# Three instead of four plain FFN chunks per layer, and an earlier first pair of weight panels, in a one-core encoder step

## The reference

```python
def swiglu(x, g, w_gu, w_down):
    gu = rmsnorm(x, g) @ w_gu
    return (jax.nn.silu(gu[..., :D_FF]) * gu[..., D_FF:]) @ w_down
```

## Time and profile before

| | us |
|---|---|
| median of 3 runs | 1208.22 |
| lowest, highest | 1208.21, 1208.87 |
| profiled execution, its own time | 1208.02 |
| its span from first to last instruction | 1206.3 |

### The profile page before, as it was taken

The page is one execution under the profiler, slowest core; times in us unless marked ns, Lnnn a source line. Parts: engine busy times, 40 slices in busy tenths (PEclk is TensorE's granted clock), DMA queues, the critical chain, the costliest instruction groups (busy, mean ns, idle before and its releaser), DMA issues.

```text
span 1206.3 us, 22717 instructions
## 1 busy us (share of the span) xinstructions
PE 1197.1 (99%) x8853; PEld 1152.8 (96%) x8853; DVE 979.7 (81%) x1585; ACT 641.6 (53%) x1136; POOL 78.5 (7%) x111
## 2 busy tenths in 40 slices
PE   8999999999999999999999999999999999999998
PEld 8998999999999999999987887899999999999998
DVE  5777458999999999976674777557999999999973
ACT  6657335455555555545672567434555555455543
POOL 2000000002001000102001100000001000100200
PEclk9999999999999999999999999999999999999999
DMA  7343222236334433526434110333134433532533
GB/s 249 108 140 105 71 78 83 74 89 136 106 88 113 121 97 91 133 80 173 137 107 140 57 41 2 105 88 88 53 101 115 120 97 94 130 105 80 131 85 105
DMA packets 195242, 124.08 MB, mean 103 GB/s; under 512 B 6339, under 2 KB 185891, under 8 KB 194880
## 3 DMA queue, kind: packets, MB, share of 16 engines
q1 hardware_dynamic: 183904, 103.30, 28.9%
q0 software_dynamic: 11040, 19.27, 7.4%
q10 hardware_dynamic: 192, 0.06, 0.0%
HBM read 106.70 MB, written 7.94 MB: 95 GB/s over the span
## 4 chain that ended last, share of the span: by engine, by line
PE 93%; DVE 3%; ACT 1%; DMA 1%; issue 1%; SPq 0%; DVEq 0%; ACTq 0%
PE ACCP L2016 28%; PE ACCP L2037 24%; PE MISC L2037 23%; PE ACCP L2173 3%; PE ACCP L2196 3%; PE ACCP L2366 2%; PE ACCP L2341 2%; PE MISC L2055 1%; PE MISC L2302 1%; PE MISC L2315 1%; DMA XR<-in_x_prompt 1%; PE MISC L2061 1%; PE ACCP L2078 1%; PE ACCP L2092 1%; DMA PC<-PC 0%
## 5 line engine op out<-in xcount | busy, mean ns | idle before, releaser
L1179 ACT ACTIVATE WH<-RAW 128x1024 fp32r<-128x1024 f32 (+2 forms) x149 | 144.2, 968 | 145.8 <-PE ACCP L2016 93.5
L1197 ACT ACTIVATE EH<-SB 128x1024 fp32r<-128x1024 f32 (+1 forms) x116 | 112.5, 970 | 163.2 <-DVE SB L1568 82.8
L1543 DVE TENSOR_TENSOR WL<-RAW,WH 128x1024 fp32r<-128x1024 f32 (+2 forms) x148 | 165.8, 1120 | 30.8 <-ACT WH L1179 29.7
L1574 DVE TENSOR_TENSOR EL<-SB,EH 128x1024 fp32r<-128x1024 f32 (+1 forms) x116 | 128.7, 1109 | 5.5 <-ACT EH L1197 3.7
L2037 PE MATMUL MISC<-BH,EH 128*128 128x288 f32 x360 | 106.7, 296 | 0.0
L2037 PE MATMUL ACCP<-BH,EH 128*128 128x288 f32 x360 | 106.6, 296 | 0.0
L2037 PE MATMUL MISC<-BL,EH 128*128 128x288 f32 x360 | 106.2, 295 | 0.0
L2037 PE MATMUL ACCP<-BL,EH 128*128 128x288 f32 x360 | 106.2, 295 | 0.0
L2037 PE MATMUL ACCP<-BH,EL 128*128 128x288 f32 x360 | 105.8, 294 | 0.0
L2037 PE MATMUL MISC<-BH,EL 128*128 128x288 f32 x360 | 105.8, 294 | 0.0
L2016 PE MATMUL ACCP<-XH,WH 128*128 128x288 f32 x480 | 104.1, 298 | 0.0
(11 more groups left out here) (411 smaller groups left out, 3432.0 us busy)
## 6 DMA issues: line engine op xcount, KB each, us to landing
RAW<-in_w_gu SPq DMA_DIRECT2D x88, 512.0 KB, 4.1
RAW<-in_w_down SPq DMA_DIRECT2D x48, 384.0 KB, 4.1
RAW<-in_w_in SPq DMA_DIRECT2D x16, 512.0 KB, 4.2
RAW<-in_w_mem_kv SPq DMA_DIRECT2D x16, 512.0 KB, 3.8
RAW<-in_w_out SPq DMA_DIRECT2D x16, 512.0 KB, 3.8
X<-PC POOLq DMA_DIRECT2D x48, 144.0 KB, 3.2
RAW<-in_w_down SPq DMA_DIRECT2D x16, 256.0 KB, 3.0
RAW<-in_w_kv SPq DMA_DIRECT2D x8, 512.0 KB, 3.6
```

Source lines behind the costliest of these rows:

```text
L1179: a.activation(panel_in(WH, w % SPLIT_SLOTS, p), panel_in(RAW, p % RAW_SLOTS, p), ACT.Copy).then_inc(split_ready(w, True)[0], 1)
L1197: a.activation(EH[:, first:first + n, 0:nh], mixtures(s)[:, first:first + n, 0:nh], ACT.Copy).then_inc(block_hi, n)
L1543: v.tensor_tensor(panel_in(WL, w % SPLIT_SLOTS, p), panel_in(RAW, p % RAW_SLOTS, p), panel_in(WH, w % SPLIT_SLOTS, p), ALU.subtract).then_ ...
L1574: v.tensor_tensor(EL[:, first:first + n, 0:nh], mixtures(s)[:, first:first + n, 0:nh], EH[:, first:first + n, 0:nh], ALU.subtract).then_in ...
```

## The change

`LEADS` becomes 3, so chunk 3 is made by a pair: a layer has six plain panels and one more pair, and the first stretch of pairs is now chunks 3, 4, 5, 6. The panels of the first pair are loaded behind the second plain panel (`load_first`), and they keep their two RAW slots until the first pair is split; the four plain panels after them take turns in the other two slots (`slot_of`). Three of the four mixtures of the first pair move to the front of the FFN's preparation on DVE, ahead of the first `prepare_scale`, and the fourth stands behind the second `prepare_scale` (`prepare_fourth`; its place in FIRST_SB overlaps ACC, which the norm's sum reads). The mixing of the first two hidden chunks (`mix_blocks`, `blocks_hi`, `blocks_lo`) leaves the plain stage: it goes to the second pair, that of chunks 2 and 3 to the third pair, that of 4 and 5 to the fourth pair. The low splits of the tokens (`lo`) move up; the seventh, `token_lo(6)`, goes into the first pair's step between the third and the fourth low split of its weights.

```diff
-    LEADS = 4
+    LEADS = 3
...
-                   (1, 0): [("mix", 3), ("mix", 6), ("hi", 1), ("hi", 2)],
-                   (1, 1): [("lo", 0), ("lo", 1), ("hi", 3), ("hi", 4)],
-                   (2, 0): [("lo", 2), ("lo", 3), ("blocks", k0), ("hi", 5), ("hi", 6)],
-                   (2, 1): [("lo", 4), ("lo", 5), ("pair", count["pair"]), ("blocks_hi", k0)],
-                   (3, 0): [("lo", 6), ("blocks_lo", k0)], (3, 1): []}
+                   (1, 0): [("mix", 3), ("mix", 6), ("hi", 1), ("hi", 2), ("lo", 0)],
+                   (1, 1): [("lo", 1), ("lo", 2), ("hi", 3), ("hi", 4)],
+                   (2, 0): [("lo", 3), ("lo", 4), ("hi", 5), ("hi", 6)],
+                   (2, 1): [("lo", 5)]}
...
                     steps.append(r_step)
+                    add("prepare_pair", k=count["pair"], s=r_step.s)
                     add("prepare_scale", layer=layer, k=0)
                     add("prepare_scale", layer=layer, k=1)
+                    add("prepare_fourth", k=count["pair"])
...
+                if (j, e) == (0, 1):
+                    first_pair = take("panel", 2)
+                    panel_shape.extend([(KC, P)] * 2)
+                    raw_free.extend([("pair", count["pair"])] * 2)
+                    add("load_first", p=first_pair, view=gate_of(LEADS), ys=up_of(LEADS))
...
+        for n in range(2):
+            slot_of[first_pair + 4 + n] = (first_pair + 2 + n) % RAW_SLOTS
...
-            if n == 1:
-                k = k0 + LEADS // 2 - 1
+            if n in (1, 2):
+                k = k0 + n - 1
...
-                if p >= RAW_SLOTS:
-                    sp.wait_ge(*raw_released(p - RAW_SLOTS))
+                if raw_before[p] is not None:
+                    sp.wait_ge(*raw_released(raw_before[p]))
...
                 elif s.kind == "prepare_pair":
                     first = steps_of_pair[s.k]
+                    dve.wait_ge(sq_free, s.s)
                     mix_1(first)
                     mix_3(first)
                     mix_2(first)
-                    mix_4(first)
+                elif s.kind == "prepare_fourth":
+                    mix_4(steps_of_pair[s.k])
...
                         dve.wait_ge(panel_used, s.before.q + 1)
-                        for n in range(4):
+                        for n in range(3):
                             mix_lo(s, n, 1)
+                        token_lo(s.layer, NB - 1)
+                        mix_lo(s, 3, 1)
                         mix_lo_22(s)
```

More of the change, by code:

```diff
@@ L160, in encoder_kernel @@
     panel_shape, splits, raw_free = [], [], []
+    slot_of = {}
     units_before, sq_of_norm, job_of_wide, branch_bank = {}, {}, [], {}
@@ L337, in feed_forward @@
         for n, (which, j, part) in enumerate(order):
-            i, p, w = take("pair"), take("panel", 2), take("split")
+            i, w = take("pair"), take("split")
             nk = KC if which == "gu" else PARTS[part][1] - PARTS[part][0]
-            panel_shape.extend([(nk, P)] * 2)
+            if n:
+                p = take("panel", 2)
+                panel_shape.extend([(nk, P)] * 2)
+                raw_free.extend([("pair", i)] * 2)
+            else:
+                p = first_pair
             splits.append(("pair", p, i))
-            raw_free.extend([("pair", i)] * 2)
             prev = steps_of_pair[i - 1] if n else None
@@ L360, in feed_forward @@
                 h=layer * FC + j if which == "gu" else None, prev=prev, nxt=n + 1 < len(order),
-                alone=n == 0, bank=n % 2, side=count["acc"] % 2, before=steps[-1] if n == 0 else None,
+                alone=n == 0, bank=n % 2, side=count["acc"] % 2, before=last_lead if n == 0 else None,
                 m=count["job"], g=count["acc"], made=made, k=k,
@@ L832, in moving_of @@
             return {"x": (XH, XL, xl_ready, T), "y": (HH, HL, yl_ready, T)}[kind]
+        raw_slot, raw_before, users = [], [], [[] for _ in range(RAW_SLOTS)]
+        for p in range(len(panel_shape)):
+            slot = slot_of.get(p, p % RAW_SLOTS)
+            raw_slot.append(slot)
+            raw_before.append(users[slot][-1] if users[slot] else None)
+            users[slot].append(p)
         def panel_in(slots, slot, p):
@@ L1041, in _ @@
                         sp.dma_start(yp[:, 2:TT, D - P:D], YST[1][:, 2:TT]).then_inc(y_last_stored, 16)
-                elif s.kind == "pair":
+                elif s.kind == "load_first" or s.kind == "pair" and not s.alone:
                     load(s.p, s.view)
@@ L1539, in split_lo, with token_lo @@
                     gate = WH[:, w % SPLIT_SLOTS]
-                    v.tensor_tensor(gate[:, :, FH:2 * FH], panel_in(RAW, p % RAW_SLOTS, p), gate[:, :, 0:FH],
+                    v.tensor_tensor(gate[:, :, FH:2 * FH], panel_in(RAW, raw_slot[p], p), gate[:, :, 0:FH],
                                     ALU.subtract).then_inc(lo_ready, 1)
                     return
-                v.tensor_tensor(panel_in(WL, w % SPLIT_SLOTS, p), panel_in(RAW, p % RAW_SLOTS, p),
+                v.tensor_tensor(panel_in(WL, w % SPLIT_SLOTS, p), panel_in(RAW, raw_slot[p], p),
                                 panel_in(WH, w % SPLIT_SLOTS, p), ALU.subtract).then_inc(split_ready(w, False)[0], 1)
+            def token_lo(layer, k):
+                dve.wait_ge(xmixed, 4 * (layer + 1))
+                dve.wait_ge(xc_hi, NB * layer + k + 1)
+                v.tensor_tensor(BL[:, k], BT[:, k], BH[:, k], ALU.subtract).then_inc(xc_lo, 1)
             def mix_1(s):
@@ L1933, in _ @@
                 elif s.kind == "prepare_lo":
-                    dve.wait_ge(xmixed, 4 * (s.layer + 1))
-                    dve.wait_ge(xc_hi, NB * s.layer + s.k + 1)
-                    v.tensor_tensor(BL[:, s.k], BT[:, s.k], BH[:, s.k], ALU.subtract).then_inc(xc_lo, 1)
-                elif s.kind == "prepare_blocks":
-                    mix_blocks(s.k)
-                elif s.kind == "prepare_blocks_lo":
-                    blocks_lo(s.k)
+                    token_lo(s.layer, s.k)
                 elif s.kind == "prepare_pair":
                     first = steps_of_pair[s.k]
+                    dve.wait_ge(sq_free, s.s)
                     mix_1(first)
```

12 lines of the change are left out of this document (6 added, 6 removed).

## The result

| | before | after |
|---|---|---|
| median of 9 runs, us | 1208.02 | 1211.24 |
| lowest, highest | 1207.29, 1208.90 | 1210.63, 1211.69 |
| profiled execution: own time, span | 1208.02, 1206.3 | 1211.69, 1210.0 |

The ratio after to before is 1.0027, with a 95% interval of 1.0017 to 1.0038: slower by 0.27%, 3.2 us. 1211.3 was predicted, in a range of 1208.5 to 1212.8. The profiled execution of after is the highest of its nine runs.

The account below looks back on a forecast made before the run. DVE, not PE, was taken to set the first stretch of pairs. Layer 0's 1.19 + 0.49 and layer 1's 0.89 + 0.49 gave +3.06 us; on the median of 1208.22 that is 1211.3 us, range 1208.5 to 1212.8.

Parts of the forecast that it names:

- Rival A: PE sets the time; DVE's lateness ends no PE wait: saving 2 x 1.58 us gives 1205.1; chance 0.13.
- The chunk's move: Layer 0: PE swaps 12.78 us for an 11.20 us pair, yet the first down pair comes 1.19 us later.
- Mixtures and loads at no cost: Before layer 0's first scale: 3.00 us of DVE idle hides three mixtures (1.9 us); panels land some 8 us early.
- Rival D: Panels land too late for the wait, mixtures push the scales by up to 1.9 us: 1211.3 to 1215; chance 0.02.
- Two intervals of 12.70: After the first pair's cross: two pairs with hidden mixing cost DVE 12.70 us each from cross to cross.
- rival B: DVE's 0.64 us idle takes up part of the low split, third sum ends no wait: about 1209.0; chance 0.12.
- The seventh low split: `token_lo(6)` in the middle of the first pair's step on DVE: adds 1.27 us, which nothing hides.
- Layer 0's first cross: End of the first pair's step on DVE: cross at 226.48, DVE then 1.5 us late.
- Rival C: ACT's splits come late too, 0.64 us per pair, up to 3.8 us: 1213 to 1215; chance 0.07.
- Layer 1: Layer 1's first down pair: 904.91 against 904.02, 0.89 us later; the second sum no longer meets the POOL DMA wait.
- Third sum: Fourth pair, before the first down pair: DVE makes it in place of a POOL DMA, 0.49 us more per layer.
- PE's waits: Third and fourth pair: PE waits for EL or `blocks_lo`, about 3.2 us in sum in each layer.

Follow-up runs that it names:

- the kernel with the move and without the two small terms: Changed kernel with `token_lo(6)` back in the plain stage and the fourth pair's sum by a POOL DMA: 1207.91 us, ratio to before 0.9999.
- the early half alone: Kernel before, still four plain chunks, with the first pair's panels loaded and mixed early, later panels' slots moved: 1207.68 us, ratio 1.0001.
- the early split: Changed kernel with the seventh low split, `token_lo(6)`, moved back into the plain stage: 1209.27 us.
- the next kernel: Changed kernel with the first two hidden chunks' mixing and low split on POOL, `token_lo(6)` in the plain stage, fourth pair's sum by POOL DMA: 1217.74 us.

## Why the prediction was right, point by point

**Who sets the stretch.** Right. More work on DVE there lengthens the kernel by as much, less work shortens it until ACT's order and PE's 11.20 are next, and with one mixing away PE runs three pairs without a wait. Rival A, by which PE would have saved 1.58 us a layer, is out. With it falls the 1205.1 by the rule of "Identifying the Most-Contended Engine" in the Trainium skill's "Perfetto Trace Analysis": the engine with the highest share of the whole span was not the one that set this stretch.

**The chunk's move.** Right, and clearer than I put it. The move takes 12.78 us of plain work from PE and adds one step of DVE, 12.70 us from cross to cross, so it is worth about nothing, and the kernel with the move and without the two small terms shows nothing. PE's 11.20 for a pair never enters the sum.

**Mixtures and loads at no cost.** Right. The first scale's idle is 1.20 us (about 1.1 was foreseen), no plain panel waits, the first pair begins at 213.22 (213.51), and the early half alone has the ratio 1.0001. Rival D is out.

**Two intervals of 12.70.** Right to 0.01 us, in both layers. The idle of 0.64 before the low split at 223.51 is still there, so rival B's way of making time up didn't happen.

**The seventh low split.** The sign and the size were right (1.27 us, nothing hides it), but I gave only half of the reason. It isn't only that DVE's work is consecutive: the place it left would now have cover, 0.95 us of waiting for ACT's EH, and the place it went to has none. Putting it back returns some 0.8 to 0.9 of its 1.27 in each layer, besides the wait for the DMA in layer 0.

**Layer 0's first cross.** This is the step that failed. I put it at 226.48 - 0.27 = 226.21 on this execution's clock; it came at 227.16. I had treated the POOL DMA as layer 1's affair, where the wait was listed, and there I was right that it vanishes. In layer 0 I put the wait for the landing at nothing and took no landing time at all. Before the change it landed 4.2 us after its issue there, and nobody waited. The chain of after shows the row that I left out:

```profile
219.18 7.58 DMA PC<-PC
...
227.16 0.75 DVE GU L1627
```

A landing as in layer 1 before (881.01 less 875.36, 5.65 us) would have been early enough. The 0.95 us too late is the whole of the difference in the layer's term, +2.14 for +1.19; the executions of the changed kernel differ in it (1.08 and 0.67 us of wait). Rival C's price came, 0.95 in place of 0.64, in one place of six and from a DMA, not from ACT.

**Layer 1.** +0.88 for +0.89.

**Third sum.** 0.49 a layer was predicted. The stretches behind the first down pair give 0.66 and 0.29, 0.95 for 0.98, and the runs without it 0.5 to 1.4 for both layers. The first down pair now shows the wait that I expected, 0.41 us for EL at 266.68.

**PE's waits.** Foreseen as 3.2 us a layer from the third pair on. In layer 0 PE reaches the first down pair at 262.48, where its own pace (213.22 + 11.44 + 3 x 11.20) gives 258.26, so 4.2 us late, the 3.25 and the DMA's 0.95. In layer 1, without the DMA's wait, it is 907.43 against 859.15 + 11.44 + 3 x 11.20 = 904.19, 3.24 us late. The waits listed up to there are shorter, 2.6 and 2.0 us, since a matmul is listed with 0.29 us and the next one starts 0.13 after it, so that part of each wait lies under a matmul's record. In layer 0 the waits begin one pair earlier than I said, with 0.23 us in the second pair; in layer 1 they begin in the third, as foreseen.

**The total.** That 1211.24 came so close to 1211.3 is in part luck. The four stretches behind the first scale sum to +3.97 us in the profiled execution of after, and to +3.51 in that of the changed kernel measured again, for the +3.06 predicted, mostly by the DMA that I had at nothing; and the median of before came out 0.20 lower with nine runs than with three. The interval of the ratio, 1.0017 to 1.0038, is 2.1 to 4.6 us wide in time and can't tell these sums apart.

**Still open.** It stays open why the sum's DMA in layer 0 took 7.0 to 7.6 us in the five profiled kernels that had the split in the first pair's step and issued that DMA as early as in after, and 5.2 to 5.3 in the two with three plain chunks that had it in the plain stage. In the first kind, the two panel loads are issued 0.6 and 0.2 us ahead of it, in the second 1.9 and 1.5. That loads under way go with a late sum can be seen within after: the sums of the second and third pair, of the same size and with no panel load under way, land 2.7 us after their issue in both layers. But the distance alone doesn't set the time: in layer 1 of after the loads also stand 0.6 and 0.2 us ahead, and the sum landed in 5.6; with 1.9 and 1.5 it is 4.1 to 4.2 us in layer 0 and 5.2 to 5.7 in layer 1 of kernels with four plain chunks. No run moved the loads and left the sum where it was. The DMA issues of the first pair's step, in after in layer 0, in layer 1, and with the early split in layer 0, and last the second pair's sum in layer 0 of after (median us to landing):

```profile
RAW<-in_w_gu SPq DMA_DIRECT2D x2, 512.0 KB, 6.1
PC<-PC POOLq DMA_DIRECT2D x1, 144.0 KB, 7.6
```

```profile
RAW<-in_w_gu SPq DMA_DIRECT2D x2, 512.0 KB, 4.6
PC<-PC POOLq DMA_DIRECT2D x1, 144.0 KB, 5.6
```

```profile
RAW<-in_w_gu SPq DMA_DIRECT2D x2, 512.0 KB, 4.4
PC<-PC POOLq DMA_DIRECT2D x1, 144.0 KB, 5.2
```

```profile
PC<-PC POOLq DMA_DIRECT2D x1, 144.0 KB, 2.7
```

In the first three, the later the sum, the later the loads.

## What to carry to other kernels

Work that moves from one stage to another is priced by the pace of the stage it goes to. Where that pace is another engine's (here DVE's 12.70 us a step, not PE's 11.20), the saving on the first engine never arrives, however high its busy share. Small steps that "have to go somewhere" during such a move should go to places where the pacing engine is idle for a neighbour: here one split in the wrong place, with the late DMA that came with it, and one sum by the wrong engine were the whole loss. And for every producer that a step waits for, DMAs included, compare the landing time with the new due time, also where no wait is listed now.

## What the runs showed of the hardware

- A subtraction of 2016 elements a partition held POOL for 5.63 us, the first 1.30 beside a DVE subtraction that had begun before it. The DVE subtraction that began next took 4.71 us in place of some 0.6 and ended 0.55 us behind POOL's: three of 1.90 us took 5.92, and in the next kernel four of 5.16 us took 10.05.
- When PE had waited 4.04 us for that, its granted clock was 0.50 from 218.73 to 222.00 (1.2 of 2.4 GHz), and 72 matmuls took 12.31 us in place of 9.83.
- The same accumulating DMA of 144 KB from SBUF to SBUF landed 2.7 to 7.6 us after its issue in one kernel: 2.7 with no panel load under way, and behind two loads of 512 KB issued 0.6 and 0.2 us ahead of it 5.6 in one layer and 7.6 in the other.
